# Dense feed-forward of a streaming encoder step: gate and up products turned round, the weight block stationary and 384 tokens moving

## The chip, the cores and the metric

The kernel runs on one core of a Trainium2 chip. The metric is the device time of one execution in microseconds, as the median of a few runs; smaller is better. A profiled execution gives a trace of every engine, which is what the rows below are from.

## What is computed

The program is one step of a 2-layer hybrid encoder for 256 prompt tokens and 8 x 16 sample tokens, 384 tokens in all, which stand as three tiles of 128. The change is in the dense feed-forward of the first layer. Cut to it, the reference is:

```python
D_MODEL = 1024
D_FF = 11 * D_MODEL // 4          # 2816

def swiglu(h, wg, wu, wd):
    return (jax.nn.silu(h @ wg) * (h @ wu)) @ wd

# layer 0:  x = x + swiglu(rms_norm(x), ffn_w_gate, ffn_w_up, ffn_w_down)
```

## The kernel before

TensorE (PE) multiplies a stationary operand of 128 x 128, which it loads first (PEld), with a moving operand of up to 512 columns, and sums over the partitions into one of eight banks of PSUM. To come close to fp32 the dense part splits every operand into a high and a low part (fp32r) and makes three matmuls of each product, high x high, high x low and low x high (`matmul3`, L963 to L965). ScalarE (ACT) makes the high part by a copy, VectorE (DVE) the low part by a subtraction.

The dense part (`dense_steps`, one for each engine) is a loop of two iterations, each over half of the 2816 features: 1408, or 11 blocks of 128 (`FFK`). In an iteration:

- Gate and up: three chunks of 512, 512 and 384 features (`FF_CHUNKS`). For each chunk gate, then up: the stationary operand is a block of the normalized activation (`hT_parts`, features of the model on partitions, 128 tokens), the moving operand the weight slab. The result has tokens on the partitions, one bank for each tile of tokens (gate banks 0 to 2, up banks 3 to 5). ACT takes the silu of gate into `acts` (L1485), DVE multiplies it by up (L1913).
- Since the down product needs features on the partitions, `turn_acts` transposes `acts` on PE, block by block, into banks 6 and 7 (L911, 33 transposes), where ACT and DVE take the high and the low part (L720, L724) into `actT`. The turn of chunk 0 stands behind the products of chunk 1, that of chunk 1 behind chunk 2, that of chunk 2 inside the down product.
- Down: two column halves, three groups of blocks each (`FF_GROUPS`), three tiles; DVE adds the result to `x` (L1924).

Weights come by 18 slabs of up to 1 MB an iteration. SP issues the load of a slab into one of three places of `ring` once the slab three before it there is split; ACT (`split_high`, L711) and DVE (`split_low`, L715) split it into one of three pairs of buffers, once PE has read what lay there. Each engine works in the order written. ACT and DVE go through one list, `events`, in which the split of slab s stands behind all bank drains up to the job that reads slab s-3 last.

Of the kernel before, what the change touches and what calls it, by code (L numbers as in the profile page):

```python
# [31 lines left out]
NT = 3  # L32
# [265 lines left out]

def dense_jobs():

    jobs, small = [], 0
    for c in range(4):
        if c < 3:
            for kind in ("gate", "up"):
                jobs += [((kind, c, t), (3 * (kind == "up") + t,), "a" if kind == "gate" else "v") for t in range(NT)]
        if c:
            for t in range(NT):
                jobs.append((("aT", c - 1, t), (T[small % 2],), "v"))
                small += 1
# [45 lines left out]
def hybrid_encoder(nc, a, o, scratch):  # L355
# [13 lines left out]
    with ExitStack() as ctx:  # L369
        def sem(name):  # L370
            return ctx.enter_context(nc.semaphore(name))
# [127 lines left out]
        assert f.at <= split0  # L499

        oT_parts = [hT_parts[0], cut(arena_r[:, NT * D:2 * NT * D], k=KC)]
        acts = cut(mem_kv[:, 0:2 * NT * 512], s=2 * NT)
        f.at = 0
        Y = parts(D, k=1)
        S = cut(arena[:, f.at:f.at + NT * P], t=NT)
# [103 lines left out]
        s_S = sem("slot_matrix_ready")  # L609
        s_units = sem("units_ready")  # L610
        s_xlast = sem("last_x_ready")

        def wait_filled(eng, *key):

# [7 lines left out]
        class Loop:  # L622
# [129 lines left out]
        half_ffn = Loop("ffn", dense_jobs(), dense_slabs(), 2, ring_slots[0:3], ("aT",), len(dense_slabs()),  # L752
                        (0, 0, 0))
        routed = Loop("routed", routed_jobs(), routed_slabs(), NE, ring_slots + kv_slots, ("gather", "down"),
                      12, (0, 2, 3))
# [132 lines left out]
        def _(pe):  # L888
# [99 lines left out]
            def dense_steps(L):  # L988

                with pe.Fori(0, L.n) as i:  # L990
                    at_ = [0]

                    def group(kind, c, left, g, groups, w):
                        k0, nk = groups[g]
                        wt = L.slab(pe, i, at_[0])
                        at_[0] += 1
                        for t in range(NT):
                            if g == 0:
                                L.begin(pe, i, kind, c, t)
                            out = bank[L.bank[(kind, c, t)][0]][:, 0:w]  # L1000
                            for k in range(k0, k0 + nk):
                                ins = matmul3(out, [q[:, k, t * P:(t + 1) * P] for q in left],
                                              [q[:, k - k0, :] for q in wt], k == 0,
                                              g == len(groups) - 1 and k == k0 + nk - 1)
                            if g == len(groups) - 1:
# [10 lines left out]
                    for c in range(3):  # L1016
                        for kind in ("gate", "up"):
                            for g in range(2):
                                group(kind, c, hT_parts, g, halves, FF_CHUNKS[c][1])
                        if c:  # L1020
                            turn_acts(c - 1)
# [432 lines left out]
        def _(act):  # L1454
# [21 lines left out]
            def dense_steps(L):  # L1476
                with act.Fori(0, L.n) as i:
                    for key in L.events:
                        if key[0] == "split":
                            L.split_high(act, i, key[1])  # L1480
                        elif key[0] == "gate":
                            _, c, t = key
                            w = FF_CHUNKS[c][1]
                            L.wait_filled(act, i, *key)
                            L.emptied_by(A(acts[:, NT * (c % 2) + t, 0:w], bank[t][:, 0:w], ACT.Silu), *key)  # L1485
                        elif key[0] == "aT":
                            _, c, t = key
                            k0, nk = FF_GROUPS[c]
                            L.high_part(act, i, actT[0][:, k0:k0 + nk, t * P:(t + 1) * P],
                                        bank[L.bank[key][0]][:, 0:nk * P].rearrange("p (k n) -> p k n", k=nk), *key)  # L1490

            def routed_step(i):
                L = routed
# [356 lines left out]
        def _(dve):  # L1850
# [52 lines left out]
            def dense_steps(L):  # L1903
                with dve.Fori(0, L.n) as i:
                    for key in L.events:
                        if key[0] == "split":
                            L.split_low(dve, i, key[1])
                        elif key[0] == "up":
                            _, c, t = key
                            at_ = acts[:, NT * (c % 2) + t, 0:FF_CHUNKS[c][1]]  # L1910
                            L.wait_filled(dve, i, *key)
                            L.wait_emptied(dve, i, "gate", c, t)
                            L.emptied_by(V.tensor_tensor(at_, bank[3 + t][:, 0:FF_CHUNKS[c][1]], at_, ALU.mult), *key)  # L1913
                        elif key[0] == "aT":
                            _, c, t = key
                            k0, nk = FF_GROUPS[c]
                            at_ = (slice(None), slice(k0, k0 + nk), slice(t * P, (t + 1) * P))
                            L.low_part(dve, i, actT[1][at_], bank[L.bank[key][0]][:, 0:nk * P].rearrange(
                                "p (k n) -> p k n", k=nk), actT[0][at_], *key)
# [41 lines left out]
            for l in range(DEPTH):  # L1961
# [199 lines left out]
                if l % 2:  # L2161
                    for t in range(NT):
                        dve.wait_ge(s_gpart, t + 1)
                        st.did(V.tensor_tensor(h_parts[1][:, t, :], htok[:, t, :], h_parts[0][:, t, :].bitcast(F32),
                                               ALU.subtract))
                    route(dve, st)
                    routed.prime(V.memset(full[:, 13:14], 0.0), "v")
                    units(dve, routed_step)
                    V.memset(full[:, 3:4], 0.0).then_inc(s_xlast, 1)
                else:  # L2170
                    half_ffn.prime(V.memset(full[:, 13:14], 0.0), "v")
                    dense_steps(half_ffn)
            for t in range(NT):
                norm_row(3 * DEPTH, t)
# [186 lines left out]
```

## Time and profile before

| | us |
|---|---|
| median of 3 runs | 1991.74 |
| the three runs | 1990.19, 1991.74, 1993.62 |
| span of the profiled execution | 1990.5 |
| of it, first iteration of the dense loop, from its first matmul | 518.98 to 675.10 |
| second iteration, to its last matmul | 675.10 to 834.73 |

The runs give no time of the profiled execution beside its span; the median lies 1.2 us above the span. In the rows below a start is in us from the start of the span; a matmul's busy time is longer than the distance to the next matmul's start, since they are pipelined.

### The profile page before, as it was taken

The numbers are of one execution on the slowest core, as the hardware profiler recorded it, in microseconds if no ns is written. First come the engines' busy times: TensorE is split into PE (matmuls) and PEld (weight loads), VectorE is DVE, ScalarE is ACT, GpSimd is POOL, SyncE is SP. The second block draws the span as 40 slices with busy tenths as digits, with TensorE's granted clock in tenths as the row PEclk, the third lists the DMA queues.
The fourth block names the chain that finished last, engine by engine and source line by source line (L and its number), as shares of the span: only waits on it lengthen the run. The fifth ranks groups of instructions, "written<-read, shape, count | busy, mean of one in ns | idle before, by whom it ended". The sixth has DMA issues, their size and how long they took to land.

```text
span 1990.5 us, 20071 instructions
## 1 busy us (share of the span) xinstructions
PE 1775.2 (89%) x7598; PEld 1222.8 (61%) x7598; DVE 791.9 (40%) x1140; ACT 609.7 (31%) x802; POOL 124.2 (6%) x243
## 2 busy tenths in 40 slices
PE   6998789878798998899977997789999999999997
PEld 3454545645678788644545475478667776667764
DVE  1611323233432333326034133246544565445653
ACT  1113112322422322210230232224443554435542
POOL 2230110000000000213002000000000000000000
PEclk9999889999899998999988999978999999999998
DMA  7534234053532333342531423536878887788873
GB/s 236 162 117 146 91 98 148 32 200 139 178 108 75 127 107 114 105 120 85 185 113 40 147 106 111 228 138 222 269 265 288 280 289 257 265 299 269 296 252 132
DMA packets 174553, 340.28 MB, mean 171 GB/s; under 512 B 6890, under 2 KB 48124, under 8 KB 174224
## 3 DMA queue, kind: packets, MB, share of 16 engines
q1 hardware_dynamic: 162224, 316.17, 46.8%
q0 software_dynamic: 3920, 12.58, 2.2%
q10 hardware_dynamic: 8352, 10.75, 1.6%
q8 instruction: 39, 0.64, 0.1%
q14 instruction: 18, 0.15, 0.0%
HBM read 329.43 MB, written 11.90 MB: 171 GB/s over the span
## 4 chain that ended last, share of the span: by engine, by line
PE 83%; DVE 7%; ACT 6%; issue 2%; DMA 1%; POOL 1%; ACTq 0%; SPq 0%; DVEq 0%; POOLq 0%
PE bank L924 19%; PE bank L963 12%; PE bank L964 12%; PE bank L965 12%; PE bank L1045 10%; PE bank L911 5%; PE bank L1064 3%; PE bank L941 2%; PE bank L1394 2%; DVE arena_parts L715 2%; ACT arena_parts L711 1%; PE bank L1092 1%; ACT arena L1460 1%; PE bank L1365 1%; DMA ring<-in_w_in 1%
## 5 line engine op out<-in xcount | busy, mean ns | idle before, releaser
L963 PE MATMUL bank<-arena_parts,features_parts 128*128 128x512 f32 (+1 forms) x960 | 375.8, 391 | 32.5 <-DVE arena_parts L715 21.6
L964 PE MATMUL bank<-arena_parts,features_parts 128*128 128x512 f32 (+1 forms) x960 | 369.8, 385 | 0.0
L715 DVE TENSOR_TENSOR arena_parts<-ring,arena_parts 128x2048 fp32r<-128x2048 f32 (+1 forms) x116 | 247.2, 2143 | 125.2 <-ACT arena_parts L711 125.2
L924 PE MATMUL bank<-ring,features_T 128*128 128x512 f32 (+1 forms) x672 | 273.7, 569 | 1.2 <-ACT features_T L1460 1.2
L711 ACT ACTIVATE arena_parts<-ring 128x2048 fp32r<-128x2048 f32 (+1 forms) x116 | 206.8, 1795 | 114.9 <-PE bank L965 114.1
L965 PE MATMUL bank<-arena_parts 128*128 128x512 f32 (+1 forms) x612 | 240.2, 392 | 0.0
L963 PEld LDWEIGHTS bank<-arena_parts,features_parts 128*128 128x128 f32 x960 | 184.6, 192 | 70.3 <-issue 16.6
L924 PEld LDWEIGHTS bank<-ring,features_T 128*128 128x128 f32 x672 | 128.8, 193 | 142.5 <-issue 138.1
L964 PEld LDWEIGHTS bank<-arena_parts,features_parts 128*128 128x128 f32 x960 | 184.7, 192 | 30.4
L1460 ACT ACTIVATE arena<-bank 128x512 f32<-128x512 f32 (+3 forms) x160 | 88.0, 562 | 373.7 <-PE bank L924 202.9
L965 PE MATMUL bank<-arena_parts,features_parts 128*128 128x512 f32 (+1 forms) x480 | 181.3, 378 | 0.0
L1045 PE MATMUL bank<-ring,arena 128*128 128x512 f32 x300 | 133.1, 596 | 5.8 <-ACT arena L1513 5.8
L911 PE MATMUL bank<-consts,arena 128*128 128x128 f32 (+1 forms) x526 | 85.8, 302 | 54.8 <-DVE arena L1858 15.7
L965 PEld LDWEIGHTS bank<-arena_parts 128*128 128x128 f32 x612 | 118.9, 194 | 23.5
L724 DVE TENSOR_TENSOR arena_parts<-bank,arena_parts 128x512 fp32r<-128x512 f32 (+1 forms) x38 | 24.9, 668 | 237.7 <-ACT arena_parts L720 237.7
L911 PEld LDWEIGHTS bank<-consts,arena 128*128 128x128 f32 (+1 forms) x526 | 63.5, 152 | 86.2 <-issue 34.7
L924 PE MATMUL bank<-ring,memT 128*128 128x512 f32 x256 | 115.7, 613 | 0.0
L965 PEld LDWEIGHTS bank<-arena_parts,features_parts 128*128 128x128 f32 x480 | 90.7, 189 | 14.8
L1045 PEld LDWEIGHTS bank<-ring,arena 128*128 128x128 f32 x300 | 55.4, 190 | 70.4 <-issue 62.2
L2186 POOL TENSOR_SCALAR stat<-stat 128x1 f32<-128x1 f32 x21 | 10.4, 495 | 1373.5 <-ACT arena L1465 1369.5
L715 DVE TENSOR_TENSOR arena_parts<-mem_kv,arena_parts 128x2048 fp32r<-128x2048 f32 (+1 forms) x40 | 80.9, 2025 | 20.0 <-ACT arena_parts L711 19.2
L924 PEld LDWEIGHTS bank<-ring,memT 128*128 128x128 f32 x256 | 50.3, 198 | 62.0 <-issue 61.9
(272 smaller groups left out, 1878.4 us busy)
## 6 DMA issues: line engine op xcount, KB each, us to landing
ring<-in_moe_w_up SPq DMA_DIRECT2D x40, 1024.0 KB, 5.1
ring<-in_moe_w_down SPq DMA_DIRECT2D x30, 1024.0 KB, 5.5
ring<-in_w_in SPq DMA_DIRECT2D x20, 1024.0 KB, 5.7
ring<-in_moe_w_gate SPq DMA_DIRECT2D x20, 1024.0 KB, 5.2
mem_kv<-in_moe_w_gate SPq DMA_DIRECT2D x20, 1024.0 KB, 5.4
ring<-in_cache_mem_k SPq DMA_DIRECT2D x16, 1024.0 KB, 6.4
ring<-in_cache_mem_v SPq DMA_DIRECT2D x16, 1024.0 KB, 5.9
ring<-in_moe_w_gate SPq DMA_DIRECT2D x20, 768.0 KB, 4.7
```

The lines of the kernel that those rows point to most:

```text
L711: nc.scalar.activation(self.part(s, 0), self.raw(s), ACT.Copy).then_inc(self.high, 1)
L715: nc.vector.tensor_tensor(self.part(s, 1), self.raw(s), self.part(s, 0).bitcast(F32), ALU.subtract).then_inc(self.split, 1)
L911: return nc.tensor.transpose(out, src, ident[0:src.shape[0], 0:src.shape[0]])
L924: ins = nc.tensor.matmul(out[:, 0:w], left(k, t), wt[:, k - k0, :], start=(g == 0 and k == k0), stop=(g == len(groups) - 1 and k == k0 + n ...
L941: ins = nc.tensor.matmul(b[:, 0:w], hT_at(k, t), wt[k // 4][:, k % 4, :], start=(k == 0), stop=(k == KC - 1))
L963: nc.tensor.matmul(out, left[0], right[0], start=start, stop=False)
L964: nc.tensor.matmul(out, left[0], right[1], start=False, stop=False)
L965: return nc.tensor.matmul(out, left[1], right[0], start=False, stop=stop)
L1045: ins = nc.tensor.matmul(out, left[:, k, :], wt[:, k - k0, :], start=start, stop=stop)
L1064: ins = nc.tensor.matmul(b[:, j * P:(j + 1) * P], h_parts[low][:, t, k * P:(k + 1) * P], S_r[:, t, :], start=(t == 0 and low == 0), stop=( ...
L1394: ins = nc.tensor.matmul(b[g:g + 32, 0:256], qxb[:, 4 * hp + i, 2 * r + n2, :], kTs[:, n2, 4 * hp + i, :], start=(i == 0), stop=(i == 3))
L1460: st.emptied(A(out, in_, ACT.Copy), *key)
```

## The change

Gate and up change their operands: the stationary one is a block of the weights (128 x 128), the moving one is the activation, all 384 tokens. The result is then a block of 128 features on the partitions by 384 tokens, which is what the down product takes: `turn_acts`, its 33 transposes and its job "aT" go. Gate block f goes to bank 6 or 7, up block f to bank 3 or 4. A slab of gate or up is now 256 features wide with all 1024 rows (two blocks; the last one), where it was 512 wide with 512 rows; there are still 18 slabs. `acts` has four places of 384 columns. After DVE's product, ACT copies the high part from `acts` to `actT`, and DVE takes the low part once both blocks of a pair have their high part; a new semaphore `s_act` counts the blocks done, and PE waits on it ahead of each group of the first down half.

```diff
 def dense_jobs():
-    jobs, small = [], 0
-    for c in range(4):
-        if c < 3:
-            for kind in ("gate", "up"):
-                jobs += [((kind, c, t), (3 * (kind == "up") + t,), "a" if kind == "gate" else "v") for t in range(NT)]
-        if c:
-            for t in range(NT):
-                jobs.append((("aT", c - 1, t), (T[small % 2],), "v"))
-                small += 1
+    jobs = []
+    for c0 in range(0, FFK, 2):
+        pair = range(c0, min(c0 + 2, FFK))
+        jobs += [(("gate", f), (6 + f % 2,), "a") for f in pair]
+        jobs += [(("up", f), (3 + f % 2,), "v") for f in pair]
     jobs += [(("down", c, t), (3 * c + t,), "v") for c in range(2) for t in range(NT)]
...
 def dense_slabs():
-    for c, (c0, w) in enumerate(FF_CHUNKS):
+    for f in range(0, FFK, 2):
+        n = min(2, FFK - f)
         for kind in ("gate", "up"):
-            for half in range(2):
-                out.append((kind, 4 * half, 4, c0, w, (kind, c, 0 if half == 0 else NT - 1)))
+            out.append((kind, 0, KC, f * P, n * P, (kind, f + n - 1)))
...
 # TensorE
+                    def features(kind, first):
+                        wt = L.slab(pe, i, at_[0])
+                        at_[0] += 1
+                        for f in range(first, min(first + 2, FFK)):
+                            out = L.begin(pe, i, kind, f)[:, 0:TOK]
+                            for k in range(KC):
+                                ins = matmul3(out, [q[:, k, (f - first) * P:(f - first + 1) * P] for q in wt],
+                                              [q[:, k, :] for q in hT_parts], k == 0, k == KC - 1)
+                            ins.then_inc(L.filled, 1)
...
-                    def turn_acts(c):
-                        for t in range(NT):
-                            L.wait_emptied(pe, i, "up", c, t)
-                            b = L.begin(pe, i, "aT", c, t)
-                            for j in range(FF_GROUPS[c][1]):
-                                ins = turn(b[:, j * P:(j + 1) * P], acts[:, NT * (c % 2) + t, j * P:(j + 1) * P])
-                            ins.then_inc(L.filled, 1)
...
-                            if (c, g) == (0, 2):
-                                turn_acts(2)
                             if c == 0:
-                                L.wait_emptied(pe, i, "aT", g, NT - 1)
-                            group("down", c, actT, g, FF_GROUPS, 512)
+                                pe.wait_ge(s_act, i * FFK + (FFK + FF_GROUPS[g][0] + FF_GROUPS[g][1]))
+                            down(c, g)
 # ScalarE
+                            act.wait_ge(s_act, i * FFK + (FFK + max(f - 3, 0)))
+                            L.emptied_by(A(acts[:, f % 4, :], bank[L.bank[key][0]][:, 0:TOK], ACT.Silu), *key)
+                        elif key[0] == "up":
+                            f = key[1]
+                            L.wait_emptied(act, i, *key)
+                            A(actT[0][:, f, :], acts[:, f % 4, :], ACT.Copy).then_inc(L.high_out, 1)
 # VectorE
+                            L.emptied_by(V.tensor_tensor(at_, bank[L.bank[key][0]][:, 0:TOK], at_, ALU.mult), *key)
+                            for g in ((f - 1, f) if f % 2 else (f,) if f == FFK - 1 else ()):
+                                dve.wait_ge(L.high_out, i * FFK + g + 1)
+                                V.tensor_tensor(actT[1][:, g, :], acts[:, g % 4, :], actT[0][:, g, :].bitcast(F32),
+                                                ALU.subtract).then_inc(s_act, 1)
```

Line numbers of the changed kernel are three to six lower on PE, ACT and DVE (L960 to L962 are its `matmul3`). On PE, where the up product of chunk 1 ended and chunk 2 began, before (the number behind bank is that of the PSUM bank; L681 and L704 work out what a wait is compared with):

```order
L965 MATMUL bank5<-arena_parts_49 128x512
L681 REGISTER_ALU
L911 MATMUL bank6<-consts,mem_kv 128x128 x4
L681 REGISTER_ALU
L911 MATMUL bank7<-consts,mem_kv 128x128 x4
L681 REGISTER_ALU
L911 MATMUL bank6<-consts,mem_kv 128x128 x4
L704 REGISTER_ALU
L681 REGISTER_ALU
L963 MATMUL bank0<-arena_parts_49,features_parts_50 128x384
```

And in the changed kernel on PE, from the last matmul of gate block 1 to the first of up block 0, the handing over from one slab and bank to the next:

```order
L962 MATMUL bank7<-features_parts_50,arena_parts_49 128x384
L701 REGISTER_ALU
L678 ISA
L960 MATMUL bank3<-features_parts_50,arena_parts_49 128x384
L961 MATMUL bank3<-arena_parts_49 128x384
```

The three transposes that shared two banks are gone; between two blocks stand only the waits for the slab and for the bank.

On ACT, the work of one pair of blocks in the changed kernel (L1480 silu of gate, L708 split of a slab, L1484 the new copy of the high part):

```order
L1480 ACTIVATE mem_kv<-bank6 128x384
L673 REGISTER_ALU
L1480 ACTIVATE mem_kv<-bank7 128x384
L708 ACTIVATE arena_parts_49<-ring 128x2048
L678 REGISTER_ALU
L1484 ACTIVATE arena_parts_49<-mem_kv 128x384
L678 REGISTER_ALU
L1484 ACTIVATE arena_parts_49<-mem_kv 128x384
L706 REGISTER_ALU
L673 REGISTER_ALU
L708 ACTIVATE arena_parts_49<-ring 128x2048
```

The copies read `acts` in `mem_kv`, where those of before (L720) read a bank of PSUM; a split still stands behind each kind's drains.

## Rows read from the trace of the kernel before

**Rows 1.** The page: span, and the chain that ended last by engine.

```profile
span 1990.5 us, 20071 instructions
...
PE 83%; DVE 7%; ACT 6%; issue 2%; DMA 1%; POOL 1%; ACTq 0%; SPq 0%; DVEq 0%; POOLq 0%
```

**Rows 2.** Busy time by stretch, the loop's two iterations (stretch, length, then engines).

```profile
core 0: us, PE busy (x) PEld busy (x) DVE busy (x) ACT busy (x) POOL busy (x), PEclk, DMA share, GB/s
518.98:675.10 156.12, 147.57 (x663) 124.60 (x663) 49.37 (x40) 42.36 (x38) 0.00 (x0) 0.96 0.34 112
675.10:834.73 159.63, 148.03 (x663) 125.23 (x663) 52.38 (x42) 40.43 (x39) 0.80 (x3) 0.96 0.34 115
```

**Rows 3.** Six stretches between products, busy time by stretch: first, last, sum.

```profile
588.34:593.04 4.70, 1.61 (x13) 1.37 (x12) 3.65 (x4) 2.46 (x3) 0.00 (x0) 0.97 0.55 194
...
802.03:805.32 3.29, 1.20 (x9) 0.73 (x8) 1.58 (x3) 1.36 (x3) 0.00 (x0) 1.00 0.00 0
sum 26.11, PE 9.54 PEld 7.66 DVE 18.23 ACT 12.56 POOL 0.00; mean PE 1.59 PEld 1.28 DVE 3.04 ACT 2.09 POOL 0.00
```

**Rows 4.** The chain of waits through the first of them (start, length, what).

```profile
588.36 1.49 ACT arena_parts L711
...
591.55 0.69 DVE arena_parts L724
592.25 0.04 issue
592.29 0.75 PE bank L911 x4
593.04 0.32 PE bank L963
```

**Rows 5.** Busy time by stretch: products behind the breaks, and a long one after.

```profile
593.04:596.24 3.20, 3.20 (x11) 3.20 (x11) 0.69 (x1) 0.60 (x1) 0.00 (x0) 0.52 0.90 324
625.15:626.85 1.70, 1.70 (x5) 1.32 (x5) 0.69 (x1) 0.60 (x1) 0.00 (x0) 0.50 0.89 304
751.57:756.69 5.12, 5.12 (x18) 5.12 (x17) 0.69 (x1) 0.60 (x1) 0.00 (x0) 0.51 0.52 200
784.14:787.13 2.99, 2.99 (x8) 2.34 (x8) 0.69 (x1) 0.60 (x1) 0.00 (x0) 0.50 0.75 259
596.20:619.90 23.70, 23.70 (x136) 23.66 (x134) 6.73 (x4) 6.57 (x6) 0.00 (x0) 1.00 0.24 78
```

**Rows 6.** Timeline of PE: ends of a run of 512 columns, then of 384.

```profile
525.06 0.39 PE L963 MATMUL bank<-arena_parts,features_parts 128*128 128x512 f32 x1
...
587.93 0.40 PE L965 MATMUL bank<-arena_parts 128*128 128x512 f32 x1
...
596.44 0.34 PE L963 MATMUL bank<-arena_parts,features_parts 128*128 128x384 f32 x1
...
619.72 0.34 PE L965 MATMUL bank<-arena_parts 128*128 128x384 f32 x1
```

**Rows 7.** Groups of instructions of the dense loop, shapes apart (count, busy, mean ns).

```profile
L963 PEld LDWEIGHTS bank<-arena_parts,features_parts 128*128 128x128 f32 x288 | 56.5, 196 | 18.6 <-issue 10.3
...
L715 DVE TENSOR_TENSOR arena_parts<-ring,arena_parts 128x2048 fp32r<-128x2048 f32 x23 | 52.3, 2290 | 63.9 <-ACT arena_parts L711 63.9
L711 ACT ACTIVATE arena_parts<-ring 128x2048 fp32r<-128x2048 f32 x22 | 41.7, 1908 | 55.6 <-PE bank L965 55.6
...
L1485 ACT ACTIVATE mem_kv<-bank 128x512 f32<-128x512 f32 x12 | 7.2, 599 | 52.8 <-PE bank L965 52.8
...
L1913 DVE TENSOR_TENSOR mem_kv<-bank,mem_kv 128x384 f32<-128x384 f32 x6 | 3.1, 552 | 8.0 <-PE bank L965 8.0
L1485 ACT ACTIVATE mem_kv<-bank 128x384 f32<-128x384 f32 x6 | 3.0, 492 | 23.4 <-PE bank L965 23.4
```

**Rows 8.** The chain of waits where the second iteration begins.

```profile
674.86 0.24 PE bank L965
...
675.75 2.28 DVE arena_parts L715
678.03 0.12 issue
678.15 0.79 PE bank L963
```

**Rows 9.** DMA issues: tensor, count, KB each, median us to landing.

```profile
ring<-in_cache_attn_k SPq DMA_DIRECT2D x4, 1024.0 KB, 5.3
...
ring<-in_ffn_w_gate SPq DMA_DIRECT2D x8, 1024.0 KB, 6.5
```

More of the change, by code:

```diff
@@ L501, in hybrid_encoder @@
         oT_parts = [hT_parts[0], cut(arena_r[:, NT * D:2 * NT * D], k=KC)]
-        acts = cut(mem_kv[:, 0:2 * NT * 512], s=2 * NT)
+        acts = cut(mem_kv[:, 0:4 * TOK], s=4)
         f.at = 0
@@ L611, in hybrid_encoder @@
         s_xlast = sem("last_x_ready")
+        s_act = sem("ffn_activation_parts_ready")
         def wait_filled(eng, *key):
@@ L751, in hybrid_encoder @@
         kv_slots = [mem_kv[:, k * SLAB:(k + 1) * SLAB] for k in range(2)]
-        half_ffn = Loop("ffn", dense_jobs(), dense_slabs(), 2, ring_slots[0:3], ("aT",), len(dense_slabs()),
+        half_ffn = Loop("ffn", dense_jobs(), dense_slabs(), 2, ring_slots[0:3], ("up",), len(dense_slabs()),
                         (0, 0, 0))
@@ L991, in dense_steps, with down @@
                     at_ = [0]
-                    def group(kind, c, left, g, groups, w):
-                        k0, nk = groups[g]
+                    def features(kind, first):
[7 more added lines that the diff above has]
+                            ins.then_inc(L.filled, 1)
+                    def down(c, g):
+                        k0, nk = FF_GROUPS[g]
                         wt = L.slab(pe, i, at_[0])
@@ L998, in group @@
                             if g == 0:
-                                L.begin(pe, i, kind, c, t)
-                            out = bank[L.bank[(kind, c, t)][0]][:, 0:w]
+                                L.begin(pe, i, "down", c, t)
+                            out = bank[L.bank[("down", c, t)][0]][:, :]
                             for k in range(k0, k0 + nk):
[L1002 to L1005, printed above, removed]
+                                ins = matmul3(out, [q[:, k, t * P:(t + 1) * P] for q in actT],
+                                              [q[:, k - k0, :] for q in wt], k == 0, k == FFK - 1)
+                            if g == 2:
                                 ins.then_inc(L.filled, 1)
-                    def turn_acts(c):
-                        for t in range(NT):
-                            L.wait_emptied(pe, i, "up", c, t)
-                            b = L.begin(pe, i, "aT", c, t)
-                            for j in range(FF_GROUPS[c][1]):
-                                ins = turn(b[:, j * P:(j + 1) * P], acts[:, NT * (c % 2) + t, j * P:(j + 1) * P])
-                            ins.then_inc(L.filled, 1)
-                    for c in range(3):
+                    for first in range(0, FFK, 2):
                         for kind in ("gate", "up"):
[L1018 to L1021, printed above, removed]
+                            features(kind, first)
                     for c in range(2):
                         for g in range(3):
-                            if (c, g) == (0, 2):
-                                turn_acts(2)
                             if c == 0:
-                                L.wait_emptied(pe, i, "aT", g, NT - 1)
-                            group("down", c, actT, g, FF_GROUPS, 512)
+                                pe.wait_ge(s_act, i * FFK + (FFK + FF_GROUPS[g][0] + FF_GROUPS[g][1]))
+                            down(c, g)
             def routed_step(i):
@@ L1481, in dense_steps @@
                         elif key[0] == "gate":
-                            _, c, t = key
-                            w = FF_CHUNKS[c][1]
+                            f = key[1]
                             L.wait_filled(act, i, *key)
[L1485 to L1490, printed above, removed]
+                            act.wait_ge(s_act, i * FFK + (FFK + max(f - 3, 0)))
+                            L.emptied_by(A(acts[:, f % 4, :], bank[L.bank[key][0]][:, 0:TOK], ACT.Silu), *key)
+                        elif key[0] == "up":
+                            f = key[1]
+                            L.wait_emptied(act, i, *key)
+                            A(actT[0][:, f, :], acts[:, f % 4, :], ACT.Copy).then_inc(L.high_out, 1)
             def routed_step(i):
@@ L1908, in dense_steps @@
                         elif key[0] == "up":
-                            _, c, t = key
-                            at_ = acts[:, NT * (c % 2) + t, 0:FF_CHUNKS[c][1]]
+                            f = key[1]
+                            at_ = acts[:, f % 4, :]
                             L.wait_filled(dve, i, *key)
[L1912 to L1919, printed above, removed]
+                            L.wait_emptied(dve, i, "gate", f)
+                            L.emptied_by(V.tensor_tensor(at_, bank[L.bank[key][0]][:, 0:TOK], at_, ALU.mult), *key)
[3 more added lines that the diff above has]
+                                                ALU.subtract).then_inc(s_act, 1)
                         elif key[0] == "down":
@@ L2171, in _ @@
                     half_ffn.prime(V.memset(full[:, 13:14], 0.0), "v")
+                    V.memset(full[:, 14:15], 0.0).then_inc(s_act, FFK)
                     dense_steps(half_ffn)
```

## The prediction

> **What bounds the kernel now.** I read the chain that ended last first: 83% of it is PE [rows 1], so what PE neither computes nor waits for is not worth a look. Then the stretches of the dense loop: 156.1 us for the first iteration, 159.6 us for the second [rows 2], 315.75 us together, with ACT and DVE busy a third of it or less and the DMA engines 0.34. Only PE's stream and its holes count.
>
> The stream first. Between 525.06 and 587.93 lie 272 starts of 512-column matmuls (by the program's order the 16th and the 288th of the loop): 62.87 / 272 = 0.2311 us from one to the next. Between 596.44 and 619.72 lie 131 starts of 384 columns (13th and 144th): 23.28 / 131 = 0.1777 us [rows 6]. Both runs cross changes of slab, and the first of bank too, without a hole. An iteration has 288 matmuls of 512 and 144 of 384 for gate and up, and 198 of 512 for down (2 x 11 x 3 x 3): 66.6 + 25.6 + 45.8 = 137.9 us. The other 18.2 and 21.7 us are holes and time at a low clock.
>
> The holes are where `turn_acts` stands. PE transposes two tiles into banks 6 and 7, and the third has to wait until bank 6 is emptied. In the chain, ACT is then in the split of a slab (1.49 us), DVE takes its low part only at 591.55, the last four transposes end at 593.04, and the products have stood since 588.34 [rows 4]. There are six such stretches, three in each iteration, 26.1 us in all [rows 3]; the one inside the down product is shorter (3.3 us), as no split is in its way. Behind four of them the products run at a granted clock of 0.50 to 0.52 (1.2 GHz) for 3.20, 1.70, 5.12 and 2.99 us, while the long run is at 1.00 (2.4 GHz) [rows 5]. PE had done little but wait and transpose before each fall.
>
> **The change part by part.** *The transposes go*, with all that lies around them: 26.1 us. The products behind them then follow at once, at the full clock. At the low clock a 384-column matmul takes 0.32 us (3.20 us for 10 starts), so 44% of 3.20 and 5.12 us is lost: 3.7 us. Taking 0.427 us for 512 columns (2.99 us for 7 starts), 46% of 1.70 and 2.99 us: 2.2 us. Together 32.0 us. The first down matmul behind a hole also starts some 0.25 us late; that is left in the rounding.
>
> *The stream gets a little longer.* Gate and up have the same products and the same number of columns, but as 528 matmuls of 384 (11 blocks x 2 x 8 x 3) in place of 288 of 512 and 144 of 384: 528 x 0.1777 = 93.8 against 92.2 us, 1.7 us more in an iteration, 3.3 in both. Down is as before. Weight loads rise from 432 to 528; they lie under the matmul before, of which more below.
>
> The Trainium skill, TensorE: Matmul & The Clock Gate, section Back-to-back issue gap, gives a distance of N / 2.4 + 2.5 ns at the full clock, 162.5 ns for 384 columns and 215.8 for 512. By that the stream would grow by 0.3 us an iteration and the change would bring an estimated 2.8 us more. The rows have 15 ns more at either width, and the sum goes by them.
>
> *ACT and DVE.* The silu and the product of 384 columns take 0.49 and 0.55 us [rows 7]. The new copy reads SBUF, which no row of this width shows: at least 384/2048 of the split's 1.91, 0.36 us, and at most the 0.60 us of a 512-column silu. I take 0.5, near the silu of its own width. The low part likewise: from 384/2048 of 2.29, 0.43 us, to the 0.69 us of DVE's step in the chain [rows 4]; I take 0.55, the product's. A pair of blocks then costs ACT 4 x 0.5 + 2 x 1.91 = 5.8 us and DVE 4 x 0.55 + 2 x 2.29 = 6.8 us, while PE needs 96 x 0.1777 = 17.1 us for it. That cover hides them. Now the order: after up of a pair ends, at T, DVE multiplies (T + 0.55), ACT copies (T + 1.05) and splits the next slab (T + 3.0), behind which DVE's low part of the slab ends at T + 5.3; its low parts of the blocks fit in between. Mid-loop PE needs that slab two slabs of 8.5 us later. The tightest is the first down slab, behind gate and up of the odd 11th block, half slabs of 24 matmuls: PE needs it at T + 8.5, 3.2 us later than it is there. The last activation block is ready 1.6 us after its up product, and PE reaches it only in the third down group, two groups of 36 x 0.2311 = 8.3 us later. Banks: gate f takes the bank of gate f-2, whose silu is some 12 us old. So I cost the new waits at nothing; uncovered, the tightest would cost what it is late, once an iteration.
>
> *DMA.* Slabs of gate and up now come in 1024 pieces of 1 KB, not 512 of 2 KB. The cached keys have that form (8 rows of 256 floats on 128 partitions) and land in 5.3 us at the median, no later than the 6.5 of the gate slabs now [rows 9]; and a slab is issued when the one three before it is split, 5.3 us behind a slab's end, while its own split is due three slabs of 8.5 us later: 20 us for the load. Nothing.
>
> *What stays.* At the turn of an iteration DVE adds the last tile to `x`, then splits the first slab: PE stops at 675.10 and goes on at 678.15 [rows 8], at the low clock for some 3 us. The changed loop has the same order there, and the same first slab size, and so has the loop's start. This is what is late next.
>
> **The sum.** 32.0 - 3.3 = 28.7, with the late first matmuls 29.0 us. I add up the old iterations in the same way as a proof: stream, holes, low clock and turn give about 0.5 us more than each of them has, so the sum may be 1 us too high; I leave it at 29. The profiled span of 1990.5 would become 1961.5, and as the median stood 1.2 us above the span, 1962.7.
>
> **The rivals.**
> - *The holes move to the slabs.* If ACT's or DVE's list runs late (each now waits for the other once for every block, with splits queued behind), PE would find the first down slab late. Twice the margin again, 3.2 us in each iteration, plus the clock that falls behind it, would leave 1962.7 + 6.4 + 3 = 1972. For it: the new waits are in line. Against: neither engine is busy for more than 7 of 17 us.
> - *A hole at each handing over.* PE now passes 22 banks and 18 slabs, some 34 places in an iteration. The chain shows 0.12 us between a release and the start of PE [rows 8]; at each place that is 34 x 2 x 0.12 = 8.2 us, 1971. Against: the runs of rows 6 cross such places with none.
> - *The weight load no longer hides*, which ends on the other side. A load is 0.196 us [rows 7], and in the 384 run it is busy 23.66 of 23.70 us [rows 5]: nothing is left. If the load of a block of the slab, rather than of the activation, let each of the 1056 matmuls start later, 29.0 / 1056 = 0.027 us, a seventh of a load, would use up the gain; a whole one would cost 203 us, 2166 in all. Against: low parts of the slab buffers' own arena are loaded in the run (L965) at the same distance.
>
> The Trainium skill, same page, section The mechanism, states that a weight load overlaps matmuls in flight only when its row group differs, which would be this last rival in full. No row bears it out: all loads here take the whole array, and the distance of 0.2311 us is less than the load and the columns in turn.
>
> **How the numbers follow.** The forecast has 0.82, and a range of its own of 1959.5 to 1966: the runs before lay 3.4 us apart, and the proof left 1 us. The moved holes have 0.08, a hole at each place 0.07, the bare weight load 0.03. The range of 1959 to 1970 takes in the forecast and the milder half of the two in between, and leaves out the last. Within 0.2%, 4 us, a measurement of this kernel can hardly tell a change. All but the last case are faster by more than that; a little goes to no change for a late queue worse than I priced. Faster 0.95, same 0.02, slower 0.03.
>
> **What would show it.** Right: no transposes and no `aT` in the loop; PE's starts 0.178 us apart through all of gate and up; the loop some 287 us long with holes only at its start, turn and, some 0.2 us, between the down halves; the clock at 1.00 from 525 to the turn. Wrong: an idle entry of PE ahead of the matmuls that waits for DVE's split or for `s_act`; starts wider than 0.2 us; a granted clock below 0.95 inside gate and up.

## The result, and the profile after

| | us |
|---|---|
| changed kernel, median of 4 runs (1954.40 to 1956.85) | 1955.49 |
| kernel before, median of the same comparison | 1991.70 |
| ratio, with its 95% interval | 0.982 (0.9806 to 0.9834) |
| span of the profiled execution | 1952.2 |

The kernel is 36.2 us faster, where I had forecast 29, and the time lies 3.5 us below the range. The device time lies 1.9 to 2.2 us above the span in the runs where both are known.

The page of the changed kernel: the slices of 49 us, busy tenths and granted clock. The dense loop is in slices 11 to 17; the chain's shares are within one point of those before [rows 1].

```profile
PE   6998789877799999999878987879999999999996
...
PEclk9999889999899999999989999969999999999998
...
PE 83%; DVE 7%; ACT 5%; issue 2%; DMA 1%; POOL 1%; ACTq 0%; SPq 0%; DVEq 0%; POOLq 0%
```

Busy time by stretch in the changed kernel: the two iterations, then the low clock of the loop's start, the first 3 us behind the turn, and 85 us of gate and up.

```profile
514.73:655.36 140.63, 140.28 (x726) 131.82 (x726) 49.90 (x44) 43.34 (x42) 0.00 (x0) 0.98 0.39 124
655.36:796.54 141.18, 137.79 (x726) 129.32 (x726) 52.94 (x46) 41.40 (x43) 0.80 (x3) 1.00 0.40 130
...
658.40:661.40 3.00, 3.00 (x17) 3.00 (x18) 3.00 (x2) 0.00 (x0) 0.00 (x0) 1.00 0.61 166
525.00:609.80 84.80, 84.80 (x487) 84.80 (x486) 32.89 (x31) 28.32 (x31) 0.00 (x0) 1.00 0.32 103
...
516.00:520.00 4.00, 4.00 (x14) 4.00 (x13) 2.99 (x2) 0.00 (x0) 0.00 (x0) 0.50 0.99 325
```

And the first 3 us behind the turn in the kernel before:

```profile
678.15:681.15 3.00, 3.00 (x7) 2.42 (x8) 3.00 (x2) 0.19 (x1) 0.00 (x0) 0.50 0.65 179
```

The reader is to set the first two of the changed kernel against [rows 2]: 140.63 + 141.18 = 281.8 us in place of 315.75, 33.9 us less, of the 36.2. PE is busy to within 0.35 us of the first iteration. Gate and up run in one piece at a clock of 1.00. The half clock is left at the loop's start alone; behind the turn, where before it was there too (0.50, 7 matmuls in 3.00 us), the clock is at 1.00 and 17 matmuls stand in 3.00 us.

The ends of the 384-column run on the changed kernel's timeline of PE, as in [rows 6], and its groups of instructions for the pieces that no row of before showed.

```profile
524.15 0.34 PE L960 MATMUL bank<-features_parts,arena_parts 128*128 128x384 f32 x1
...
609.47 0.34 PE L962 MATMUL bank<-features_parts,arena_parts 128*128 128x384 f32 x1
```

```profile
L1910 DVE TENSOR_TENSOR arena_parts<-mem_kv,arena_parts 128x384 fp32r<-128x384 f32 x22 | 12.2, 554 | 2.4 <-ACT arena_parts L1484 1.2
L1484 ACT ACTIVATE arena_parts<-mem_kv 128x384 fp32r<-128x384 f32 x22 | 11.6, 526 | 69.4 <-DVE mem_kv L1907 69.4
```

The 40th and the 528th start lie 85.32 us apart, 0.1748 us from one to the next, where [rows 6] gave 0.1777. The copy takes 0.53 us (I took 0.5), the low part 0.55 (0.55).

What PE waited for in the whole loop, and the chain at the two places that are left: the change of down halves, and the turn.

```profile
PE bank L960 <- DVE arena_parts L712: 10.1, 4, 6.4
```

```profile
627.98 0.24 PE bank L962
628.22 0.02 issue
628.25 1.93 ACT arena_parts L708
630.17 0.02 issue
630.20 2.30 DVE arena_parts L712
632.50 0.12 issue
632.62 0.49 PE bank L960
...
656.00 2.28 DVE arena_parts L712
658.28 0.12 issue
658.40 0.43 PE bank L960
658.84 0.18 PE bank L961
```

Four waits, all for a split slab: the loop's start (6.4 us), the turn, and one between the down halves of each iteration, which hides under the last two tiles but for some 0.25 us. None is for an activation block or a bank. Behind the turn the first matmul takes 0.43 us and the next 0.18; before it was 0.79 and half the clock [rows 8].

### The profile page after: what moved, and what is told of

Read it like the earlier page. It is cut to its first block, busy times and chain, and to the rows that moved or that the text cites. A ratio compares the mean times of both kernels' runs of the same rounds, so it can differ in the third digit from the quotient of the medians.

```text
span 1952.2 us, 20368 instructions
## 1 busy us (share of the span) xinstructions
PE 1755.2 (90%) x7724; PEld 1234.0 (63%) x7724; DVE 793.1 (41%) x1149; ACT 611.6 (31%) x810; POOL 124.0 (6%) x243
## 4 chain that ended last, share of the span: by engine, by line
PE 83%; DVE 7%; ACT 5%; issue 2%; DMA 1%; POOL 1%; ACTq 0%; SPq 0%; DVEq 0%; POOLq 0%
PE bank L921 20%; PE bank L960 12%; PE bank L962 12%; PE bank L961 12%; PE bank L1039 10%; PE bank L908 4%; PE bank L1058 3%; PE bank L938 2%; PE bank L1388 2%; DVE arena_parts L712 2%; PE bank L1086 1%; ACT arena L1454 1%; ACT arena_parts L708 1%; PE bank L1359 1%; DVE arena L2126 1%
## 5 line engine op out<-in xcount | busy, mean ns | idle before, releaser
L712 DVE TENSOR_TENSOR arena_parts<-ring,arena_parts 128x2048 fp32r<-128x2048 f32 (+2 forms) x116 | 247.2, 2143 | 108.7 <-ACT arena_parts L708 108.7
L960 PE MATMUL bank<-arena_parts,features_parts 128*128 128x512 f32 (+1 forms) x672 | 262.8, 391 | 23.5 <-DVE arena_parts L712 12.2
L961 PE MATMUL bank<-arena_parts,features_parts 128*128 128x512 f32 (+1 forms) x672 | 258.6, 385 | 0.0
L708 ACT ACTIVATE arena_parts<-ring 128x2048 fp32r<-128x2048 f32 (+2 forms) x116 | 206.6, 1793 | 71.3 <-PE bank L962 70.5
L962 PE MATMUL bank<-arena_parts,features_parts 128*128 128x512 f32 (+1 forms) x480 | 181.7, 379 | 0.0
L961 PE MATMUL bank<-arena_parts 128*128 128x384 f32 (+1 forms) x484 | 170.6, 353 | 0.0
L960 PEld LDWEIGHTS bank<-arena_parts,features_parts 128*128 128x128 f32 x672 | 128.1, 191 | 52.1 <-DVE arena_parts L712 16.1
L961 PEld LDWEIGHTS bank<-arena_parts,features_parts 128*128 128x128 f32 x672 | 128.0, 190 | 22.1
L960 PE MATMUL bank<-features_parts,arena_parts 128*128 128x384 f32 x352 | 120.3, 342 | 9.5 <-DVE arena_parts L712 9.5
L962 PE MATMUL bank<-arena_parts 128*128 128x512 f32 x324 | 128.5, 396 | 0.0
L962 PE MATMUL bank<-features_parts,arena_parts 128*128 128x384 f32 x352 | 119.6, 340 | 0.0
L962 PEld LDWEIGHTS bank<-arena_parts,features_parts 128*128 128x128 f32 x480 | 90.6, 189 | 14.5
L961 PEld LDWEIGHTS bank<-arena_parts 128*128 128x128 f32 x484 | 91.8, 190 | 5.1
```

Source lines behind the costliest of these rows:

```text
L708: nc.scalar.activation(self.part(s, 0), self.raw(s), ACT.Copy).then_inc(self.high, 1)
L712: nc.vector.tensor_tensor(self.part(s, 1), self.raw(s), self.part(s, 0).bitcast(F32), ALU.subtract).then_inc(self.split, 1)
```

## The experiments

**The changed kernel again.** No edit.

> The changed kernel once more, word for word. Theory 1: the dense loop alone brings 33.9 us (315.75 to 281.8), of which my sum had 29.0; the rest is the distance of the gate and up matmuls (0.1748 instead of 0.1777 us, 3.0 us) and the turn of the iterations, which ran at the full clock (1.7 us); the 4.3 us by which the first profile reached the loop earlier are chance. Then the loop's length repeats within 0.5 us if the turn is at the full clock again and is 283.5 if not, its start lies anywhere from 514 to 519.5 us, and the ratio is 0.981 to 0.983. Rival: the change itself makes the part ahead of the loop shorter; then the loop starts within 0.5 us of 514.7 again and the ratio stays below 0.981.

Its loop took 281.82 us (516.83 to 798.65), the turn at the full clock; the ratio was 0.9833 (0.9805 to 0.9861), 1957.76 against 1990.73 us. The loop's length repeats to 0.02 us. Its start does not: over the profiles of all these kernels it lay between 512.4 and 521.2 us, at 519.0 and 515.3 in the two of the kernel before and from 514.7 to 518.3 in the three of the changed one. So the 4.3 us by which the first profile of the changed kernel came to the loop sooner are no effect of the change. The runs of the kernel before went from 1983 to 1999 us in this comparison.

**The kernel before without transposes.** Products as before, and ACT and DVE take the two parts straight from `acts`, so that the values of the layer are not the reference's.

```diff
-                            turn_acts(c - 1)
...
+                        elif key[0] == "up":
+                            L.wait_emptied(act, i, *key)
+                            A(actT[0][:, k0:k0 + nk, t * P:(t + 1) * P],
+                              acts[:, NT * (c % 2) + t, 0:nk * P].rearrange("p (k n) -> p k n", k=nk),
+                              ACT.Copy).then_inc(L.high_out, 1)
```

> The kernel before without its transposes: products as before (activation stationary, 512 and 384 weight columns moving), but ACT and DVE take the high and low part straight from acts, so that features and tokens stay unturned for the down product; the output of the layer is not the reference's. Theory 1: all of the gain is in the holes and the clock behind them; gate and up keep 0.2311 and 0.1778 us, and the loop takes 281.5 us with the turn at the full clock, 283.2 without: level with the changed kernel within 1.5 us. The step of my prediction that the turned stream costs 1.7 us more in an iteration would have this kernel 3.3 us below the changed one. Rival: the turning itself is worth several us: then this kernel's loop is 286 us or more.

Busy time by stretch in that kernel, its two iterations:

```profile
521.20:662.10 140.90, 140.52 (x630) 118.56 (x630) 48.94 (x41) 42.42 (x39) 0.00 (x0) 0.98 0.37 124
662.10:803.05 140.95, 137.61 (x630) 116.68 (x630) 51.94 (x42) 40.43 (x39) 0.79 (x3) 1.00 0.38 130
```

281.85 us, the changed kernel's loop to within 0.1 us, with the old products (0.1777 us for 384 columns). All of the gain is what the transposes brought with them; turning the product round only makes it possible, and neither costs nor gives. This kernel's whole time (1896.5 us) says nothing, since the routed experts behind see other data and run another number of units: behind 1000 us one group of their matmuls has 270 in place of 300.

**Transposes without waits.** 33 transposes of the identity put back in each iteration of the changed kernel.

```diff
+                        if first in (6, 8, 10):
+                            if first == 6:
+                                L.wait_emptied(pe, i, "down", 0, NT - 1, back=1)
+                            for t in range(NT):
+                                for j in range(FF_GROUPS[(first - 6) // 2][1]):
+                                    turn(bank[t][:, j * P:(j + 1) * P], ident)
```

> The changed kernel with the 33 transposes of an iteration put back on PE, of the identity, into banks 0 to 2 that stand idle there, with nobody waiting for them and nothing read from them: 12 behind blocks 6 and 7, 12 behind 8 and 9, 9 behind 10. If the six holes of 26.1 us were waits, the transposes alone cost their 0.109 us each, 66 x 0.109 = 7.2 us, loop 289 us, clock at 1.00. If transposes by themselves let the clock fall, the products behind them run at half of it for some 3 us each, 1.4 us lost at each of six places: loop 297 us.

The loop took 289.08 us (519.71 to 808.79): 7.3 us for 66 transposes, 0.11 us each, and no matmul behind one of them at the low clock. So of the six stretches' 26.1 us [rows 3] some 7 were transposing and 19 waiting, and the half clock behind them came of the waiting.

**One hole put back.** The changed kernel, with PE waiting for three dependent memsets of DVE ahead of the third down group.

```diff
+                            if (c, g) == (0, 2):
+                                turn(bank[6][:, 0:P], ident).then_inc(s_hole[0], 1)
+                                pe.wait_ge(s_hole[1], i * 3 + 3)
```

> The changed kernel with one hole put back in each iteration: ahead of the third group of the first down half PE transposes the identity once and waits for three dependent memsets on DVE of some 0.9 us each, about 3 us, where the kernel before had its third turn. Theory: what PE did earlier in the iteration decides on the clock behind the turn, since the same hole of 3.05 us there was followed by half the clock in four of four profiles with the six holes and by the full one in all without them; then one hole brings the half clock back behind the turn, and the loop takes 281.8 + 6 for the holes + 1.7 = 289.5 us, a little more if it falls behind the holes too. Rival: the turn's clock hangs on something else (the width of the products before it); then it stays at the full clock, loop 288 us.

Busy time by stretch in that kernel: hole and what follows it in the first iteration, the turn and what follows, the hole and what follows in the second.

```profile
627.40:631.38 3.98, 0.27 (x2) 0.01 (x1) 2.74 (x3) 0.00 (x0) 0.00 (x0) 0.93 0.00 0
631.97:633.20 1.23, 1.23 (x4) 0.99 (x3) 0.00 (x0) 0.00 (x0) 0.00 (x0) 0.50 0.00 0
661.90:665.23 3.33, 0.27 (x3) 0.01 (x1) 3.03 (x3) 1.91 (x1) 0.00 (x0) 0.96 0.00 0
665.23:667.50 2.27, 2.27 (x7) 2.27 (x8) 2.27 (x2) 0.00 (x0) 0.00 (x0) 0.50 0.44 109
775.40:779.38 3.98, 0.27 (x2) 0.01 (x1) 2.74 (x3) 0.00 (x0) 0.00 (x0) 1.00 0.00 0
779.38:782.00 2.62, 2.62 (x11) 2.17 (x12) 0.24 (x1) 0.24 (x1) 0.00 (x0) 1.00 0.00 0
```

The half clock is back behind the turn (0.50), after the same hole of 3.05 us that the changed kernel has there at 1.00. That is what the theory expects; that an earlier hole decides is not shown by it, and the kernel with half the width, below, speaks against it. The hole itself is followed by the half clock in the first iteration and by the full one in the second. The loop took 292.7 us, 3 more than I expected: the holes are nearly 4 us long, and the clock fell behind one of them too.

**The kernel before again.** No edit.

> The kernel before, word for word, for a second profile of it. Theory: the start of its loop lies anywhere between 514 and 521 us, its six holes and the distances (0.231, 0.178, 0.227 us) repeat within 0.1 us, and the loop takes 315 to 318 us. Open: whether its products behind the turn of the iterations start at half the clock again (as in its first profile) or at the full one (as in all four profiles of changed kernels). If at the full one, the 1.7 us that the turn gave in the first comparison were chance and no effect of the change.

Its loop took 312.79 us, 2.95 less than the first time. Busy time by stretch behind its first break, behind the first of the second iteration, behind its turn, and behind the second break of the second iteration:

```profile
589.00:592.60 3.60, 3.60 (x15) 3.60 (x14) 0.94 (x2) 0.60 (x1) 0.00 (x0) 0.53 0.95 298
747.60:749.50 1.90, 1.90 (x9) 1.90 (x8) 0.69 (x1) 0.60 (x1) 0.00 (x0) 0.50 0.91 274
675.10:677.90 2.80, 2.80 (x8) 2.15 (x7) 2.80 (x2) 0.00 (x0) 0.00 (x0) 0.50 0.83 251
...
778.80:781.80 3.00, 3.00 (x16) 2.49 (x15) 0.83 (x2) 0.60 (x1) 0.00 (x0) 1.00 0.88 270
```

The turn is at half the clock again, as it was in all profiles with holes ahead of it (the two of before, the three with other addresses below, and the one hole); it was at the full clock in all three of the changed kernel, without transposes, and with transposes without waits. But it was at half the clock in the kernel with half the width too, which has no hole ahead of it. In the second iteration the clock rose sooner behind the first break than in [rows 5], and behind the second it did not fall at all (1.00, where [rows 5] has 0.50 at 784.14): these two make up the 2.95 us. So the same break of the same program was followed by either clock.

**Addresses.** Three kernels with the products of before. In one the two parts of the activation change places; in the next the arena starts 32 bytes further on and the split buffers on multiples of 64 bytes; in the last the features tensor moves by 32 and the arena by 64 bytes.

```diff
-        hT_parts = [cut(features_r[:, :], k=KC), cut(arena_r[:, f.at - KC * TOK:f.at], k=KC)]
+        hT_parts = [cut(arena_r[:, f.at - KC * TOK:f.at], k=KC), cut(features_r[:, :], k=KC)]
```

> The kernel before with the places of the activation's two parts exchanged: the high part, which is stationary in two of three matmuls, in the arena, the low part in the features tensor. If the distance of matmuls hangs on where the stationary operand lies (down, with all operands in the arena, has 0.2267 us for 512 columns; gate and up, two thirds from the features tensor, 0.2311), gate and up should fall to 0.228 to 0.229 us for 512 and to some 0.176 for 384. If it hangs on the roles or on the order of the loop, they stay at 0.2311 and 0.1777.

```diff
+        sb("pad", 8)
-        split0 = (arena_w - NSPLIT * 2 * SLAB) // 8 * 8
+        split0 = (arena_w - NSPLIT * 2 * SLAB) // 16 * 16
```

> The kernel before with the arena 32 bytes further on and its split buffers on multiples of 64 bytes (the features tensor already starts on one). If the distance hangs on operands that start at different places within 64 bytes, gate and up become equal to down (0.2267 for 512 columns) and 384 columns take 0.174 to 0.175 us; if not, all distances stay as they are.

```diff
+        sb("pad0", 8)
         fT_ = sb("features_T", KC * TOK)
...
+        sb("pad1", 8)
```

> The kernel before with the features tensor and the arena both moved on by 32 and 64 bytes, so that all operands of the dense products start at the same place within 64 bytes (32). The run with all at 0 had 0.2333 us in gate and up and in down. If equal places within 64 bytes are what costs, gate and up and down are at 0.233 here too; if place 32 is good and 0 bad, all are near 0.227; if neither, the distance hangs on more than these bits of the address.

Mean distance of starts in ns, worked out from the timelines of PE as for [rows 6], starts at the low clock left out:

| kernel | gate and up, 512 | gate and up, 384 | down, 512 |
|---|---|---|---|
| before | 231.1 | 177.7 | 227 |
| parts exchanged | 233.3 | 177.6 | 227 |
| arena + 32 bytes | 233.3 | 175.5 | 233.3 |
| features + 32, arena + 64 | 233.3 | 175.5 | 233.3 |
| changed kernel | | 174.8 | 227 |

The same matmuls in the same order change their distance by up to 6 ns with nothing but the places of their operands. None of my three rules holds: the arena for the high part did not help, and the two kernels that I laid out to have equal places within 64 bytes give 233 ns, where the down products of before, which I took to have them too, give 227. The traces hold no addresses, so these places are my working of the layout and not shown. Which bits of the address decide stays open.

**Half the width.** Each gate and up matmul of the changed kernel cut into two of 192 columns.

```diff
+                            for h in range(2):
+                                at2 = slice(h * TOK // 2, (h + 1) * TOK // 2)
...
-                                ins = matmul3(out, [q[:, k, (f - first) * P:(f - first + 1) * P] for q in wt],
-                                              [q[:, k, :] for q in hT_parts], k == 0, k == KC - 1)
+                                    ins = matmul3(out[:, at2], [q[:, k, (f - first) * P:(f - first + 1) * P] for q in wt],
+                                                  [q[:, k, at2] for q in hT_parts], k == 0, k == KC - 1)
```

> The changed kernel with each gate and up matmul cut into two of 192 columns, 1056 in an iteration where there were 528, each with its own weight load. If the load of 0.188 us that the trace shows bounds the distance, 192 columns take 0.188 us, and gate and up 397 us in both iterations instead of 184.6: loop 494 us. If the shown duration of a load is not what bounds (transposes of 128 columns follow each other at 0.109 us with a load each), 192 columns take 0.109 us or less, gate and up 230 us, loop 327 us. Either way it tells at which width the stationary weight block would have lost.

Its timeline of PE:

```profile
559.73 0.28 PE L962 MATMUL bank<-features_parts,arena_parts 128*128 128x192 f32 x1
559.84 0.27 PE L960 MATMUL bank<-features_parts,arena_parts 128*128 128x192 f32 x1
559.95 0.28 PE L961 MATMUL bank<-arena_parts 128*128 128x192 f32 x1
```

0.112 us from one to the next, not 0.188: a weight load's shown duration is not what bounds, and a full PEld row (84.80 of 84.80 us in the changed kernel) does not tell that the loads are the limit. But 192 columns cost 64% of 384, so gate and up take 28% longer in two halves. The loop took 334.9 us (512.43 to 847.31), 19 and 22 more than in the two profiles of the kernel before, and the whole kernel 2003 us in its one run: what is a gain at 384 columns is a loss at 192.

This loop has no hole ahead of its turn: PE's waits are the same four as in the changed kernel. Busy time by stretch at its turn, hole and what follows:

```profile
678.53:681.98 3.45, 0.39 (x2) 0.01 (x1) 3.02 (x3) 1.98 (x2) 0.00 (x0) 1.00 0.03 5
681.98:684.90 2.92, 2.92 (x14) 2.92 (x15) 2.92 (x2) 0.00 (x0) 0.00 (x0) 0.52 0.65 184
```

The hole of 3.06 us is followed by half the clock, some 0.21 us from matmul to matmul in place of 0.112, with nothing but products ahead of it. So a hole earlier in the iteration is not needed for that.

**Earlier split at the turn.** ACT's and DVE's loops written out, so that the first two slabs of the second iteration are split ahead of the last two additions to `x`.

```diff
+                        if i + 1 < self.n and key == ("down", 1, 0):
+                            out += [(i + 1, ("split", 0)), (i + 1, ("split", 1))]
...
-                with dve.Fori(0, L.n) as i:
-                    for key in L.events:
+                    for i, key in L.unrolled():
```

> The changed kernel with ACT's and DVE's loop written out for both iterations, so that DVE splits the first two slabs of the second iteration ahead of its last two additions to x. PE's hole at the turn of 3.04 us should shrink to some 0.3 us, since ACT and DVE get the slab ready 4.2 us after the first of the last three tiles: 2.7 us less. Written out, ACT also loses the table load of 1.28 us ahead of the first split, so the loop starts 1.3 us sooner against the end of the norm: 4.0 us less in all, ratio about 0.979 to 0.980. If the first split waits for something else at the turn (its slab's load), the hole stays and only 1.3 us are won.

> The kernel with the earlier split once more, beside the changed one, for the interval: its loop 278.4 us long and its first split 1.4 us earlier, 4.8 us together: some 0.0024 of the ratio below that of the changed kernel, which the runs' spread of several us may hide.

> The changed kernel beside the former: loop 281.8 us, ratio 0.982 to 0.984 as in the two comparisons so far.

The first comparison gave 0.9812 (0.9779 to 0.9845), which does not stand apart from the changed kernel's. The second, side by side, gives 0.9795 (0.9781 to 0.9808) against 0.9826 (0.9813 to 0.984), 1952.72 against 1958.12 us: the intervals do not meet. The chain of the kernel with the earlier split at the turn, and its loop by stretch:

```profile
653.21 2.30 DVE arena_parts L725
655.51 0.12 issue
655.63 0.44 PE bank L973
```

```profile
515.46:793.77 278.31, 277.13 (x1452) 260.30 (x1452) 102.76 (x90) 82.95 (x83) 0.78 (x3) 0.99 0.40 129
```

The loop is 3.5 us shorter than the changed kernel's 281.85 of that comparison: 2.7 us at the turn, as expected, and 0.9 us at the loop's start, where the clock stayed at half for 3.6 us behind the first matmul in place of 5.6. Between the last start of the norm's transposes and its first start lie 5.41 us in place of 6.83; the table load of 1.28 us now stands behind the first splits. It beats both kernels.

## Why the prediction was wrong

The direction and the mechanism were right: PE's stream bounds the loop, the holes go, nothing takes their place. The size was not. In us, by the terms of the sum:

| term | forecast | shown, first pair of profiles | second pair |
|---|---|---|---|
| holes, with the late first matmuls | -26.4 | -25.8 | -25.8 |
| half clock behind them | -5.9 | -6.8 | -3.7 |
| gate and up stream | +3.3 | +0.3 | +0.3 |
| turn of the iterations | 0 | -1.6 | -1.7 |
| sum | -29.0 | -33.9 | -30.9 |

What is shown is worked out from the starts of PE's matmuls: a hole is the distance of the starts on its two sides less one undisturbed distance (231.1, 177.7 or 227 ns), and the half clock is what a run of starts takes beyond its undisturbed distances. The stream is 528 x 0.1748 = 92.3 against 92.2 us, twice. The loop is 33.9 us shorter in the first pair and 31.0 in the second, so nothing else in it changed.

*The step that failed first* is "528 x 0.1777 = 93.8 against 92.2 us, 1.7 us more in an iteration". I took the distance of 384 columns from a run with other operands in other places and gave it no bounds: the one row was taken as a price of the width. The runs show it to be one of the places too: 175.5 to 177.7 ns at this width with the products of before, and 174.8 in the changed kernel. The bound was at hand: the down products of before run 4 ns faster at 512 columns than gate and up, which I had put down at the same 0.2311 us. Over 198 of them that is 0.8 us, more than the "0.5 us more" in each iteration of my proof, which I took as a sign that the sum was too high. That the mean of the changed kernel comes from the addresses alone is not shown, since it also changes which operand is loaded.

*The second* is "What stays": the turn has the same hole of 3.05 us, and I took the half clock behind it for a part of the hole. It is not: in the twelve profiles with this hole the full clock followed in five and half the clock in seven. The theory that I wrote ahead of the run with one hole put back, that what PE did earlier in the iteration decides, does not hold either, since the kernel with half the width has no earlier hole and half the clock. What is left is when the hole begins, which differs from kernel to kernel with the length of the iteration. The clock records in the traces bear this out: they change only at moments of even spacing, and of the 34 holes of 3 to 4 us in these profiles the 8 that begin between 0.35 and 0.51 of the way from one such moment to the next kept the full clock, and the 26 that begin up to 0.33 or from 0.80 on did not. This is a count over runs made for other ends; no run moved a hole by itself, so the cause is not shown.

*The half clock behind the six holes* was 0.9 us more than forecast in the first profile of before and 2.2 us less in the second. That the first is near the forecast is in part luck, since the same breaks can be followed by either clock.

*The range* lacked both, and the spread: 33.9 us off the median of 1991.74 is 1957.8, below the lower end of 1959 already, and the 1955.49 measured lies 2.3 us lower. Of the spread the range allowed 3.4 us, where the 11 runs of the kernel before in the second comparison go over 16 us. The three comparisons give 36.2, 33.0 and 34.8 us; the loop's two pairs of profiles give 33.9 and 31.0. What lies between is within that spread, and no more of it is explained.

*The Trainium skill's formula* for the distance (TensorE: Matmul & The Clock Gate, section Back-to-back issue gap, which calls it the gap of a single matmul), which I set aside, would have come closer with its 0.3 us an iteration for the stream's growth. Both its distances are too short here: 162.5 ns against 174.8 at 384 columns, 215.8 against 227 and more at 512.

*The last rival* falls: 528 weight loads of the whole array an iteration, each shown with 0.19 us, go with matmuls 0.1748 us apart, so the loads lie under the matmuls. The rule of the Trainium skill that the prediction named beside it (TensorE: Matmul & The Clock Gate, section The mechanism), that a load overlaps matmuls in flight only where the row group differs, does not agree with that. The price of 203 us that I gave for bare loads is 207 by its own row (1056 x 0.196), which changes nothing else.

*The rivals.* No hole moved to the slabs: the first down slab was there, as the wait rows show. No hole at each handing over: in the first iteration the 488 distances from the 40th start on are even, none above 0.18 us, across 20 of the 21 changes of block. The margins of ACT's and DVE's lists held, with the copy and the low part at the prices taken.

## What to carry to other kernels

When a product's result has to be transposed for the next one, ask first whether exchanging the operands gives it the right way round; look for the gain in the waits around the transposes (19 of 26 us here), not in the transposes. Then see how wide the moving operand gets: at 384 columns the stationary weights cost nothing; cut to 192 columns they lost more than the holes had cost. A program of 192 tokens was not run. And a row's duration is the price of its shape and its place; where another row of the same shape differs (227 and 231 ns here), both are the bounds.

## What was not expected of the hardware

- The distance of equal matmuls changed between 227 and 233 ns (512 columns) and between 175.5 and 177.7 ns (384) with the places of the operands; a shift of the arena by 32 bytes, with its split buffers on multiples of 64, made the down products 6 ns slower.
- The same hole of 3.05 us was followed by half the clock in seven profiles and by the full one in five; an earlier hole is not what decides, and by the clock records it goes with when the hole begins.
- 66 transposes of 0.11 us in an unbroken stream, 9 or 12 in a row, left the clock at full; it fell behind the stretches with waits.
- A weight load is shown with 0.188 to 0.195 us even where the loads follow each other at 0.112 us.
